# Attention tiles: the next queries turned before the third value product; and products of constants at the start

## The chip, the cores and the metric

The kernel runs on one core of a Trainium2 chip. Its engines run side by side and wait for each other by semaphores: TensorE (PE in the profile; PEld is its weight load), VectorE (DVE), ScalarE (ACT), GpSimd (POOL), and SyncE (SP), whose queue issues the DMAs. The metric is the device time of one execution in microseconds; three runs of the kernel before gave 1705.12, 1705.86 and 1711.52, median 1705.86.

## The reference

One step of a two-layer decoder on 2048 prompt tokens and 64 sample tokens (8 sequences of 8), width 1024, all in fp32:

```
# layer 0 (phase A, and the first half of phase B)
h = rms_norm(x, norm_a);  a, gl, z = split(h @ w_in_a, 3)
v = a * sigmoid(gl);      c = causal depthwise conv of v, 31 taps, + b_dw
x1 = x + (silu(layer_norm(c)) * silu(z)) @ w_out_a
# shared keys and values, queries, gate (the rest of phase B; the gate in phase C)
k, v = split(rms_norm(x1, norm_kv) @ w_kv);  k = rms_norm per head
q, z = split(rms_norm(x1, norm_b) @ w_in_b); q = rms_norm per head
# layer 1 (phase C), per block of 128 queries, over its own and the block before of keys
s = q k^T / 8 - slope * distance   (causal, window 128)
p = exp(s - m) / (sum + exp(sink - m));  o = p v
y = x1 + (o * silu(z)) @ w_out_b
```

There are 16 query heads on 4 key and value heads (groups of 4 query heads), head width 64.

## The kernel before

Each engine runs a program written out in order; what stands first in an engine's program and waits holds all behind it on that engine. Three phases follow each other: A (`phase_a`, to about 600 us) projects x for layer 0 and convolves; B (to about 1064 us, with a tail beside the first attention tile) norms, projects back, and makes keys, values and queries; C (`phase_c`) is the attention over 16 tiles of 128 queries (t = 0 to 15), and the sample tokens beside tiles 6 to 13.

**The start of phase A.** SyncE issues `load_x(0)`, the broadcast of the norm's gain, `load_x(1)`, unit 0 of the weights, `load_x(2)`, unit 1; then `load_x(3)`, which waits for the first x to be turned, eight small loads, and only then `load_unit(2)`. For each tile of x, ScalarE squares it (L514), GpSimd makes the root (L471, L473), VectorE scales it in place by root and gain (`scale_x`, L610), TensorE turns it in eight instructions (`turn_x`, L705), ScalarE copies the turned tile (`cut_hi`, L520) and VectorE the remainder (`cut_lo`, L616). The weights of a unit are cut by ScalarE (`split_hi`, L526) and VectorE (`split_lo`, L620). VectorE's program has `split_lo(2)` ahead of `scale_x(3)`. TensorE's first product group follows the first two turned tiles.

**A tile of phase C**, in the order of TensorE's program (`body`, L2387), where four groups of heads kv = 0 to 3 each have scores (`qk`, L2334), a turn of the exponentials P (`turn_p`, L2342) and a value product (`pv`): `pv` first turns two pieces of the gate (L2351), for which it waits for the group before to be multiplied out (`o_done`), then waits for P (`pt_ready`) and multiplies (L2357). Between these stand the gate's projection of this tile (`z`, L121 on `c_ht`) and the output projection of the tile before (`out`, L121 on `c_ot`). The tile ends: second half of `out`, `pv` of group 2 (the third value product), `turn_p` of group 3, the turn of the next tile's queries (`turn_q`, L2258), the turn of its keys (`turn_k`, L2264), `pv` of group 3 (the fourth). The next tile begins with `qk` of its group 0, which waits for queries and keys to be copied; in tiles 6 to 13 two turns of cached keys (L2294) stand before it.

What goes on beside that: after each value product ScalarE copies the turned gate (`copy_gate`, L1894), VectorE multiplies (`gated`, L2077), and only behind that in VectorE's program stands the copy of the next group's turned P (`parted`, L2054), for which `pv` waits. ScalarE copies the turned queries (`queries`, L1865) and keys (`keys`, L1871 and L1872; two copies where the next tile is even, one where it is odd).

**Tile 0** differs: it has no `out`; the gate of the sample tokens is projected there (`decode_z`, L130), and before `turn_q(1)` TensorE waits for VectorE to read its second half (`d_dve` at 3, VectorE L2089), since both use the same bank.

Of the kernel before, what the change touches and what calls it, by code (L numbers as in the profile page):

```python
# [14 lines left out]
P = 128  # L15
D = 1024
# [17 lines left out]
LN_EPS = 1e-5  # L34
# [234 lines left out]
def phase_a(nc, io, g, ctx):  # L269
# [5 lines left out]
    with ExitStack() as reused:  # L275
# [71 lines left out]
        def sync(sp, load_first, load_gate, load_second, load_x1, load_keys):  # L347
            def load_x(t):
                after(sp, xt_done, t - 2)
                n = rows_of(t)  # L350
                sp.dma_start(x[t % 3][0:n], io.x_sample if n == DEC else token_rows(io.x_prompt, t, n)).then_inc(x_in[t % 3], 16)
# [21 lines left out]
                sp.dma_start(g.vnew_d[b * P:(b + 1) * P, :], vbuf[:, b % 2, HIST + SEQ:HIST + TOK]).then_inc(vnew_out, 16)  # L373

            load_x(0)
            sp.dma_start(gain[:, :], io.norm_a.rearrange("(a d) -> a d", a=1).broadcast_to([P, D])).then_inc(gain_in, 16)
            load_x(1)
            load_unit(0)
            load_x(2)
            load_unit(1)  # L380
# [75 lines left out]
        def gpsimd(pool):  # L456
            pool.memset(g.half[:, :], -0.5).then_inc(ident_made, 1)
            pool.memset(g.rms_eps[:, :], RMS_EPS)
            pool.memset(g.share[:, :], 1.0 / D)
            pool.memset(g.ln_eps[:, :], LN_EPS).then_inc(ident_made, 1)  # L460
            pool.memset(g.ident[:, :], 0.0).then_inc(ident_made, 1)
            pool.wait_ge(ident_made, 3)
            pool.affine_select(out=g.ident[:, :], in_=g.ident[:, :], compare_op=ALU.not_equal, fill=1.0, base=0,
                               pattern=[[-1, P]], channel_multiplier=1).then_inc(ident_made, 1)
            pool.memset(vbuf[:, 0, 0:HIST], 0.0).then_inc(hist_zero, 1)

            def rms(t):
                n, q = rows_of(t), t % 2
                pool.wait_ge(ss_ready, t + 1)
                after(pool, xs_ready, t - 1)  # L470
                pool.tensor_tensor(ms[0:n, q:q + 1], ss[0:n, q:q + 1], g.rms_eps[0:n, 0:1], ALU.add).then_inc(ms_ready, 1)  # L471
                pool.wait_ge(ms_ready, t + 1)
                pool.tensor_tensor(rstd[0:n, q:q + 1], ms[0:n, q:q + 1], g.half[0:n, 0:1], ALU.pow).then_inc(rstd_ready, 1)  # L473

            def add_product(m):

                n, i = divmod(m, PTAPS - 1)
                i += 1
                _, t0, t1 = piece(n)
                out = csum[:, slot_of(n), 0:t1 - t0]  # L480
                pool.wait_ge(prod_ready, PTAPS * n + i + 1)
                if i == 1:
                    if n in (1, 2):
                        pool.wait_ge(hist_out, 16)
                    after(pool, c_out[slot_of(n)], 16 * (n // 3 + (n == pieces - 1)))
                    pool.tensor_tensor(out, prod[:, PTAPS * n % RING, 0:t1 - t0], prod[:, (PTAPS * n + 1) % RING, 0:t1 - t0], ALU.add).then_inc(prod_added, 1)  # L486
                    return
                pool.wait_ge(prod_added, m)
                pool.tensor_tensor(out, prod[:, (PTAPS * n + i) % RING, 0:t1 - t0], out, ALU.add).then_inc(prod_added, 1)  # L489

            for t in range(4):
                rms(t)
            added = 0
            for i in range(count):
                while added < plan.adds_by[i]:
                    add_product(added)
                    added += 1
                for t in range(2, ALL - 2):
                    if plan.cut_at[t] == i:
                        rms(t + 2)  # L500
                if i == plan.state_at + 3:
                    pool.wait_ge(st_t, 2)
                    pool.memset(vbuf[:, 1, 0:HIST], 0.0).then_inc(hist_zero, 1)
            while added < pieces * (PTAPS - 1):
                add_product(added)
                added += 1
# [192 lines left out]
        def tensor(pe, turn_first, turn_back):  # L699
            def turn_x(t):  # L700
                n = rows_of(t)
                pe.wait_ge(xs_ready, t + 1)
                after(pe, lo_ready, t - 1)
                for k in range(KT):
                    last = pe.transpose(ps_t[t % 2][:, k, 0:n], x[t % 3][0:n, k * P:(k + 1) * P], g.ident[0:n, 0:n])  # L705
                last.then_inc(xt_done, 1)

            def turn_state():
                n = DB * HIST // 2
                pe.wait_ge(st_in, 32)  # L710
                pe.wait_ge(lo_ready, ALL)
                for h in range(2):
                    for k in range(KT):
                        last = pe.transpose(ps_t[h][:, k, 0:n], x[h][0:n, k * P:(k + 1) * P], g.ident[0:n, 0:n])
                    last.then_inc(st_t, 1)

            def turn_v(b):
                pe.wait_ge(v_ready, NCH * (b + 1))
                pe.wait_ge(st_copied, 2)
                cols = slice(b * P, (b + 1) * P)  # L720
                pe.transpose(flat_t[1][0:HIST + DEC, cols], vbuf[:, b % 2, SEQ:HIST + TOK], g.ident[:, :]).then_inc(vt_done, 1)

            def project_group(i, between=None):
                u, c = groups[i]
                n = CHUNKS[c]
                if i >= 4:
                    done = {GATE: sig_ready, VALUE: v_ready, ZGATE: z_copied}[kind[i - 4]]
                    pe.wait_ge(done, nth[i - 4] + 1)
                pe.wait_ge(u_lo, u + 1)
                pe.wait_ge(lo_ready, CTILES[c + 1])  # L730
                out = bank[i % 4][:, 0:n]
                for k in range(KT):
                    if k == KT // 2 and between is not None:
                        pe.wait_ge(vo_ready, 1)
                        between()
                    if k == KT // 2:
                        for t in range(ALL):
                            if plan.turn_at[t] == 2 * i + 1:
                                turn_x(t)
                    for a, e in ((0, 0), (0, 1), (1, 0)):  # L740
                        last = pe.matmul(out, wring[:, u % 3, a, k], xt[c][:, e, k, 0:n], start=(k == 0 and a == 0 and e == 0),  # L741
                                         stop=(k == KT - 1 and a == 1))
                last.then_inc(grp, 1)

            pe.wait_ge(ident_made, 4)
            for i in range(count):
                if i == 3:
                    pe.wait_ge(raw_in, 16 * (2 + VECS + 2))
                    pe.transpose(bank[3][:, 0:P], raw[:, 0], g.ident[:, :])
                    pe.transpose(bank[3][:, P:TAPS * KT], raw[0:TAPS * KT - P, 1], g.ident[0:TAPS * KT - P, 0:TAPS * KT - P])  # L750
                    pe.transpose(bank[3][:, 256:256 + VECS * KT], raw[0:VECS * KT, 2], g.ident[0:VECS * KT, 0:VECS * KT]).then_inc(cols_t, 1)
                for t in range(ALL):
                    if plan.turn_at[t] == 2 * i:
                        turn_x(t)
                if i == 3:
                    pe.wait_ge(cols_ready, 2)
                if i == plan.state_at:
                    turn_state()
                for b in range(KT):
                    if plan.vt_at[b] == i:  # L760
                        turn_v(b)
                if i == last_z(0, 4):
                    turn_back()
                project_group(i, turn_first if i == out_at[2] else None)
# [841 lines left out]
def phase_c(nc, io, g, ctx, prev):  # L1606
# [245 lines left out]
    def scalar(act):  # L1852
# [51 lines left out]
        def decode_tanh(half):  # L1904
            part = zd[:, half * HALF:(half + 1) * HALF]
            act.wait_ge(d_pe, 3 + half)
            act.activation(part, z_at[half][DEC:P], ACT.Copy).then_inc(d_act, 1)
            act.wait_ge(d_dve, 1 + 2 * half)
            act.activation(low[0], part, ACT.Tanh, scale=0.5).then_inc(d_act, 1)
# [37 lines left out]
        def body(t, r):  # L1947
# [38 lines left out]
            exps(t * KVH + 3, 1)  # L1986
            if first:
                decode_tanh(1)
            copy_gate(t * KVH + 2, 2)
            if first:  # L1990
                split(6)
            if not last:
                queries(t + 1)
                keys(t + 1, 1 - r)
            if isinstance(t, int) and t == TILES - 2:
                decode_cut()
# [256 lines left out]
    def tensor(pe):  # L2253
# [133 lines left out]
        def body(t, r):  # L2387
# [42 lines left out]
                decode_z(1)  # L2430
            else:
                out(t - 1, 1, isinstance(t, int) and t == 1)
            pv(t, 2, r, loads)
            turn_p(t, 3, 1)
            if first:
                pe.wait_ge(d_dve, 3)
            if not last:
                turn_q(t + 1)
                if not first:
                    pe.wait_ge(res_done, t * 2)  # L2440
                turn_k(t + 1, 1 - r)
# [144 lines left out]
```

## Time and profile before

| | |
|---|---|
| median of three runs | 1705.86 us |
| the profiled execution, own time | 1704.73 us |
| its span, first to last instruction | 1702.9 us |
| TensorE busy (PE), weight load (PEld) | 97%, 79% |
| VectorE, ScalarE, GpSimd busy | 75%, 46%, 38% |
| mean granted clock of TensorE | 0.992 |

The busy shares are means over phases with different limits. The chain that ended last, followed back from the end, gives 60% to TensorE and 22% to GpSimd, whose share lies in phase A; in phase C it stays on TensorE nearly throughout. Two readings of the page need care: matmuls are pipelined, so a row's duration overlaps the next row's, and the step from start to start is what an instruction costs in a stream; and an fp32 product that isn't a turn shows as two TensorE instructions.

### The profile page before, as it was taken

The numbers are of one execution on the slowest core, as the hardware profiler recorded it, in microseconds if no ns is written. First come the engines' busy times: TensorE is split into PE (matmuls) and PEld (weight loads), VectorE is DVE, ScalarE is ACT, GpSimd is POOL, SyncE is SP. The second block draws the span as 40 slices with busy tenths as digits, with TensorE's granted clock in tenths as the row PEclk, the third lists the DMA queues.
The fourth block names the chain that finished last, engine by engine and source line by source line (L and its number), as shares of the span: only waits on it lengthen the run. The fifth ranks groups of instructions, "written<-read, shape, count | busy, mean of one in ns | idle before, by whom it ended". The sixth has DMA issues, their size and how long they took to land.

```text
span 1702.9 us, 26944 instructions
## 1 busy us (share of the span) xinstructions
PE 1644.7 (97%) x10267; PEld 1349.6 (79%) x10267; DVE 1272.8 (75%) x1944; ACT 778.9 (46%) x1625; POOL 648.8 (38%) x504
## 2 busy tenths in 40 slices
PE   7999999999999988999999999978999999999998
PEld 6899888888898876888888888756777777777776
DVE  6479889898888657889889433567777777777774
ACT  6655555565554545443343333454333443333431
POOL 2489999999985304445444332200000000000000
PEclk9999999999999999999999999989999999999999
DMA  7411111121120555444454342744222233322311
GB/s 218 129 58 43 50 48 55 48 69 44 62 89 28 181 195 201 139 158 156 156 149 156 119 155 80 234 146 129 97 97 72 85 106 115 103 102 91 104 62 44
DMA packets 153722, 186.06 MB, mean 109 GB/s; under 512 B 51028, under 2 KB 116668, under 8 KB 149450
## 3 DMA queue, kind: packets, MB, share of 16 engines
q1 hardware_dynamic: 149274, 172.54, 31.8%
q10 hardware_dynamic: 4320, 11.80, 1.8%
q8 instruction: 82, 1.34, 0.3%
q14 instruction: 46, 0.38, 0.1%
HBM read 116.41 MB, written 70.72 MB: 110 GB/s over the span
## 4 chain that ended last, share of the span: by engine, by line
PE 60%; POOL 22%; DVE 7%; ACT 3%; DMA 3%; issue 3%; SPq 1%; POOLq 0%; DVEq 0%; ACTq 0%
POOL a_csum L489 21%; PE c_acc L121 19%; PE b_pso L121 15%; PE b_psq L121 9%; PE c_pso L2357 4%; PE a_ps L741 3%; DVE a_pst L639 3%; PE c_pss L2334 2%; PE c_psp L2342 2%; POOL a_csum L486 1%; PE b_pst L1510 1%; PE a_pst L705 1%; PE c_pso L2351 1%; DVE w L109 1%; PE c_pst L2258 1%
## 5 line engine op out<-in xcount | busy, mean ns | idle before, releaser
L741 PE MATMUL a_ps<-a_xt,a_wring 128*128 128x512 f32 (+3 forms) x2880 | 557.7, 354 | 9.5 <-ACT a_zo L551 6.4
L741 PEld LDWEIGHTS a_ps<-a_xt,a_wring 128*128 128x128 f32 x2880 | 495.0, 189 | 65.8 <-ACT a_zo L551 8.0
L489 POOL TENSOR_TENSOR a_csum<-a_prod,a_csum 128x704 f32<-128x704 f32 (+1 forms) x231 | 405.3, 1754 | 43.1 <-ACT a_prod L538 9.9
L639 DVE SCALAR_TENSOR_TENSOR a_pst<-a_vbuf,taps,a_pst 128x704 f32<-128x704 f32 (+1 forms) x338 | 314.1, 929 | 10.4
L538 ACT ACTIVATE a_prod<-a_vbuf,taps 128x704 f32<-128x704 f32 (+1 forms) x252 | 214.7, 863 | 166.5 <-POOL a_csum L489 154.9
L121 PE MATMUL c_acc<-w,c_ht 128*128 128x512 f32 x768 | 184.8, 396 | 3.0 <-DVE c_sz L2019 2.3
L121 PE MATMUL b_pso<-w,b_yt 128*128 128x512 f32 x768 | 182.2, 393 | 0.7 <-DVE b_yt L1312 0.7
L121 PEld LDWEIGHTS c_acc<-w,c_ht 128*128 128x128 f32 x768 | 142.8, 189 | 39.2 <-issue 10.3
L121 PEld LDWEIGHTS b_pso<-w,b_yt 128*128 128x128 f32 x768 | 141.9, 188 | 29.5 <-DVE b_yt L1312 1.1
L1886 ACT ACTIVATE c_es<-c_es 128x4 f32<-128x4 f32 x64 | 13.1, 205 | 198.4 <-DVE c_es L2044 198.4
L121 PE MATMUL b_psq<-b_w,b_ht 128*128 128x512 f32 x384 | 94.9, 403 | 4.5 <-DVE b_w L109 4.5
L1888 ACT ACTIVATE c_s<-c_s,c_nm 128x128 f32<-128x128 f32 x256 | 98.8, 387 | 0.1
L121 PE MATMUL b_pso<-w,b_ht 128*128 128x512 f32 x384 | 91.4, 394 | 3.4 <-issue 3.4
L121 PE MATMUL b_psq<-w,b_ht 128*128 128x512 f32 x384 | 91.4, 393 | 0.0
L2031 DVE SCALAR_TENSOR_TENSOR c_s<-c_dist,c_pss 128x256 f32<-128x256 f32 (+1 forms) x256 | 88.1, 406 | 2.9 <-PE c_pss L2334 2.9
L121 PEld LDWEIGHTS b_psq<-b_w,b_ht 128*128 128x128 f32 x384 | 72.7, 193 | 21.2 <-DVE b_w L109 6.3
L121 PE MATMUL c_acc<-w,c_ot 128*128 128x512 f32 x360 | 85.9, 394 | 2.9 <-issue 2.9
L1400 DVE SCALAR_TENSOR_TENSOR b_conv<-b_three,taps,b_conv 128x704 f32<-128x704 f32 x90 | 87.1, 967 | 2.0
L121 PEld LDWEIGHTS b_pso<-w,b_ht 128*128 128x128 f32 x384 | 73.0, 191 | 19.0 <-issue 3.6
L121 PE MATMUL c_acc<-b_w,c_ot 128*128 128x512 f32 x360 | 86.0, 394 | 1.1 <-issue 1.1
L121 PEld LDWEIGHTS b_psq<-w,b_ht 128*128 128x128 f32 x384 | 71.0, 188 | 15.6
L121 PEld LDWEIGHTS c_acc<-b_w,c_ot 128*128 128x128 f32 x360 | 66.4, 188 | 17.9 <-issue 3.9
(247 smaller groups left out, 2242.3 us busy)
## 6 DMA issues: line engine op xcount, KB each, us to landing
ht_d<-b_ht SPq DMA_DIRECT2D x16, 1024.0 KB, 5.0
c_ht<-ht_d SPq DMA_DIRECT2D x16, 1024.0 KB, 5.0
a_stage<-in_w_in_a SPq DMA_DIRECT2D x24, 512.0 KB, 4.2
a_x<-in_x_prompt SPq DMA_DIRECT2D x16, 512.0 KB, 3.6
b_cz<-c_d SPq DMA_DIRECT2D x16, 512.0 KB, 5.6
b_cz<-z_d SPq DMA_DIRECT2D x16, 512.0 KB, 4.1
b_x<-in_x_prompt SPq DMA_DIRECT2D x16, 512.0 KB, 4.2
x_d<-b_x SPq DMA_DIRECT2D x16, 512.0 KB, 2.6
```

What stands on the lines that cost most here:

```text
L109: dve.scalar_tensor_tensor(g.wslot[m][:, 1, k], g.stage[:, piece % g.stages], gain_of(gain, k), f32(g.wslot[m][:, 0, k]), ALU.mult, ALU.su ...
L121: last = pe.matmul(out, xt[:, a, k, 0:n], w[:, b, k], start=(k == 0 and a == 0 and b == 0), stop=(k == KT - 1 and b == 1))
L489: pool.tensor_tensor(out, prod[:, (PTAPS * n + i) % RING, 0:t1 - t0], out, ALU.add).then_inc(prod_added, 1)
L538: act.activation(prod[:, m % RING, 0:t1 - t0], vbuf[:, b % 2, t0 + k:t1 + k], ACT.Identity, scale=wcol(k, b), bias=bcol(b) if i == 0 else ...
L639: dve.scalar_tensor_tensor(part if k == DTAPS - 1 and not last else here, vbuf[:, b % 2, t0 + k:t1 + k], wcol(k, b), part if k == 0 else h ...
L741: last = pe.matmul(out, wring[:, u % 3, a, k], xt[c][:, e, k, 0:n], start=(k == 0 and a == 0 and e == 0), stop=(k == KT - 1 and a == 1))
L1400: dve.scalar_tensor_tensor(cw, win, w, cw, ALU.mult, ALU.add).then_inc(old_step, 1)
L1888: ins = act.activation(s[:, b, j], s[:, b, j], ACT.Exp, bias=nm[:, b, j:j + 1], accum_out=den[:, b, j:j + 1])
L2031: ins = dve.scalar_tensor_tensor(to, far, -slope[kv * GROUP + j], given, ALU.mult, ALU.add)
L2334: ins = pe.matmul(to, qt[rows, h // 2, part * SUB:(part + 1) * SUB], keys[:, span_of(t, part)], start=True, stop=True)
L2342: ins = pe.transpose(ps_p[:, b, j], s[:, b, j], g.ident[:, :])
L2357: ins = pe.matmul(ps_o[e * HD:(e + 1) * HD, 0:2 * P], v[:, half, kv * HD:(kv + 1) * HD], pt[:, half, 2 * e:2 * e + 2], start=(half == 0), ...
```

## The change

Two parts. In phase C, TensorE turns the next tile's queries right after the second half of `out`, ahead of the third value product, and ScalarE copies them ahead of that product's gate copy; the turn of the keys stays where it was. In phase A, TensorE multiplies a constant column (`g.share`, spread to 128x128) 22 times before the first x is there, twice after the first turned tile and seven times before the first product group; GpSimd fills that column earlier by one place, and SyncE loads the second x ahead of the gain.

```diff
@@ sync
             load_x(0)
+            load_x(1)
             sp.dma_start(gain[:, :], io.norm_a...).then_inc(gain_in, 16)
-            load_x(1)
             load_unit(0)
@@ gpsimd
-            pool.memset(g.share[:, :], 1.0 / D)
-            pool.memset(g.ln_eps[:, :], LN_EPS).then_inc(ident_made, 1)
+            pool.memset(g.ln_eps[:, :], LN_EPS)
+            pool.memset(g.share[:, :], 1.0 / D).then_inc(ident_made, 1)
@@ tensor, phase A
+            def warm(n):
+                ones = g.share[:, :].broadcast_to([P, P])
+                for _ in range(n):
+                    pe.matmul(bank[3][:, 0:P], ones, ones, start=True, stop=True)
+            pe.wait_ge(ident_made, 2)
+            warm(22)
             pe.wait_ge(ident_made, 4)
...
                         turn_x(t)
+                        if t == 0:
+                            warm(2)
+                if i == 0:
+                    warm(7)
@@ scalar, phase C
             exps(t * KVH + 3, 1)
             if first:
                 decode_tanh(1)
+            if not last:
+                queries(t + 1)
             copy_gate(t * KVH + 2, 2)
             if first:
                 split(6)
             if not last:
-                queries(t + 1)
                 keys(t + 1, 1 - r)
@@ tensor, phase C
                 out(t - 1, 1, isinstance(t, int) and t == 1)
-            pv(t, 2, r, loads)
-            turn_p(t, 3, 1)
             if first:
                 pe.wait_ge(d_dve, 3)
             if not last:
                 turn_q(t + 1)
+            pv(t, 2, r, loads)
+            turn_p(t, 3, 1)
+            if not last:
                 if not first:
                     pe.wait_ge(res_done, t * 2)
                 turn_k(t + 1, 1 - r)
```

On TensorE, at the end of a tile of phase C (c_ot: attention output; c_sz: gate; c_pt, c_v: P and values; c_q, c_kd: next queries and keys), before:

```order
L121 MATMUL c_acc<-w,c_ot 128x512 x24
L2351 MATMUL c_pso<-ident,c_sz 128x128 x2
L2357 MATMUL c_pso<-c_pt,c_v 64x256 x4
L2342 MATMUL c_psp<-ident,c_s 128x128 x4
L2258 MATMUL c_pst<-ident,c_q 128x128 x8
L2264 MATMUL c_acc<-ident,c_kd 128x128 x4
L2351 MATMUL c_pso<-ident,c_sz 128x128 x2
L2357 MATMUL c_pso<-c_pt,c_v 64x256 x4
L2334 MATMUL c_pss<-c_kt,c_qt 32x160 x16
```

Now, at the same place (the line numbers are those of the changed kernel: L2364 and L2370 are `pv`, L2355 `turn_p`, L2271 `turn_q`, L2277 `turn_k`, L2347 `qk`):

```order
L121 MATMUL c_acc<-w,c_ot 128x512 x24
L2271 MATMUL c_pst<-ident,c_q 128x128 x8
L2364 MATMUL c_pso<-ident,c_sz 128x128 x2
L2370 MATMUL c_pso<-c_pt,c_v 64x256 x4
L2355 MATMUL c_psp<-ident,c_s 128x128 x4
L2277 MATMUL c_acc<-ident,c_kd 128x128 x4
L2364 MATMUL c_pso<-ident,c_sz 128x128 x2
L2370 MATMUL c_pso<-c_pt,c_v 64x256 x4
L2347 MATMUL c_pss<-c_kt,c_qt 32x160 x16
```

The eight turns of the queries moved from between the third and the fourth value product to ahead of the third; nothing else changed place.

On TensorE at the start of the program (a_x: tiles of x; a_xt, a_wring: turned x and weights), before:

```order
L705 MATMUL a_pst<-ident,a_x_59 128x128 x8
L705 MATMUL a_pst<-ident,a_x_60 128x128 x8
L741 MATMUL a_ps<-a_xt_49,a_wring 128x256 x12
L705 MATMUL a_pst<-ident,a_x_63 128x128 x8
L741 MATMUL a_ps<-a_xt_49,a_wring 128x256 x12
L705 MATMUL a_pst<-ident,a_x_59 128x128 x8
```

Now, with the products of the constant column (share):

```order
L749 MATMUL a_ps<-share 128x128 x22
L705 MATMUL a_pst<-ident,a_x_59 128x128 x8
L749 MATMUL a_ps<-share 128x128 x2
L705 MATMUL a_pst<-ident,a_x_60 128x128 x8
L749 MATMUL a_ps<-share 128x128 x7
L741 MATMUL a_ps<-a_xt_49,a_wring 128x256 x12
L705 MATMUL a_pst<-ident,a_x_63 128x128 x8
```

The three L749 rows are new; the others stand in the order of before.

## Rows read from the trace of the kernel before

**Rows 1.** Waits of TensorE, 1175 to 1703 us: who, whom, us, times, longest
```profile
PE c_pss L2334 <- issue: 1.4, 3, 0.5
```

**Rows 2.** Timeline of TensorE at the end of tile 3: start, us, engine, line, times
```profile
1253.80 1.08 PE L2357 MATMUL c_pso<-c_pt,c_v 128*64 128x256 f32 x8
...
1255.31 1.04 PE L2258 MATMUL c_pst<-ident,c_q 128*128 128x128 f32 x8
1256.18 0.60 PE L2264 MATMUL c_acc<-ident,c_kd 128*128 128x128 f32 x4
...
1257.02 1.08 PE L2357 MATMUL c_pso<-c_pt,c_v 128*64 128x256 f32 x8
1258.57 0.78 PE L2334 MATMUL c_pss<-c_kt,c_qt 64*32 64x160 f32 x32 [0.46 <-issue]
```

**Rows 3.** Timeline of VectorE at the same place; in brackets idle time, its releaser
```profile
1255.35 0.42 DVE L2077 TENSOR_TENSOR c_sz<-c_pso,c_sz 128x256 f32<-128x256 f32 x1 [0.97 <-ACT c_sz L1894]
1255.69 1.28 DVE L2054 TENSOR_TENSOR c_pt<-c_psp,c_causal 128x512 f32<-128x512 f32 x2
```

**Rows 4.** Timeline of ScalarE at the same place
```profile
1256.38 1.11 ACT L1865 ACTIVATE c_qt<-c_pst,b_qscale 128x1024 f32<-128x1024 f32 x1 [1.06 <-PE c_pst L2258]
...
1257.87 0.60 ACT L1872 ACTIVATE c_kt<-c_acc 128x512 f32<-128x512 f32 x1
```

**Rows 5.** Timeline of TensorE at the end of tile 15, which turns no queries
```profile
1677.01 1.08 PE L2357 MATMUL c_pso<-c_pt,c_v 128*64 128x256 f32 x8
...
1679.13 0.41 PE L2351 MATMUL c_pso<-ident,c_sz 128*128 128x128 f32 x2 [0.45 <-DVE c_sz L2077]
1680.24 1.08 PE L2357 MATMUL c_pso<-c_pt,c_v 128*64 128x256 f32 x8 [0.69 <-DVE c_pt L2054]
```

**Rows 6.** Timeline of TensorE from tile 7 to 8, and from 8 to 9
```profile
1398.28 0.44 PE L2294 MATMUL c_pst<-ident,c_stg 128*128 128x128 f32 x2
1398.81 0.78 PE L2334 MATMUL c_pss<-c_kt,c_qt 64*32 64x160 f32 x32
...
1433.99 0.44 PE L2294 MATMUL c_pst<-ident,c_stg 128*128 128x128 f32 x2
1434.36 0.77 PE L2334 MATMUL c_pss<-c_kt,c_qt 64*32 64x160 f32 x32
```

**Rows 7.** Timeline of TensorE in tile 0
```profile
1141.93 0.66 PE L2342 MATMUL c_psp<-ident,c_s 128*128 128x128 f32 x4 [0.59 <-ACT c_s L1888]
1144.60 1.09 PE L2258 MATMUL c_pst<-ident,c_q 128*128 128x128 f32 x8 [2.01 <-DVE c_early L2089]
```

**Rows 8.** Windows: stretch, length, busy us (instructions) by engine, PEclk, DMA share, GB/s
```profile
8.00:15.60 7.60, 3.90 (x16) 3.12 (x16) 4.78 (x4) 5.39 (x8) 0.95 (x3) 1.00 0.92 283
15.60:20.10 4.50, 4.42 (x21) 4.46 (x22) 3.86 (x4) 2.70 (x4) 2.17 (x3) 1.00 0.53 179
...
1116.00:1126.00 10.00, 6.67 (x65) 4.36 (x63) 8.38 (x21) 3.69 (x13) 2.33 (x1) 1.00 0.39 107
1126.00:1133.00 7.00, 4.49 (x21) 3.37 (x18) 2.50 (x9) 3.02 (x13) 0.00 (x0) 0.51 1.07 304
```

**Rows 9.** Timeline of all engines, 17 to 22 us
```profile
17.23 1.07 ACT L526 ACTIVATE a_wring<-a_stage 128x1024 fp32r<-128x1024 f32 x1
...
18.38 1.89 PE L705 MATMUL a_pst<-ident,a_x 128*128 128x128 f32 x8
19.71 1.28 DVE L610 SCALAR_TENSOR_TENSOR a_x<-a_x,a_rstd,a_gain 128x1024 f32<-128x1024 f32 x1
...
21.54 1.04 PE L705 MATMUL a_pst<-ident,a_x 128*128 128x128 f32 x8
```

**Rows 10.** The load of weight unit 2 by itself: duration ns, start us, and landing
```profile
L357 SPq DMA_DIRECT2D a_stage<-in_w_in_a x1: 401/401/401, 13.4 to 13.4; - x1
...
DMA to landing us min/median/max: 3.8/3.8/3.8
```

**Rows 11.** A product with the constant column in phase B, all of the program
```profile
L1499 PE MATMUL b_psc<-share,b_cz x28: 270/273/323, 670.3 to 1039.1; 128*128 128x128 f32 x26, 128*64 128x128 f32 x2
```

## The prediction

> **What bounds the kernel now.** I read four views, in this order: the waits of TensorE in phase C, the timelines of three engines at the end of one tile, the same place in the last tile, and then the start and tile 0 by timeline and windows. From tile 1 on phase C is a stream of TensorE: of waits for the next tile's first scores the trace lists three, 1.4 us together [rows 1], and there is no slack in which a later wait could be lost. A microsecond that TensorE waits at a tile's end is therefore a microsecond of the kernel. What matters is who is late there.
>
> At the end of tile 3 the third value product starts at 1253.80 and the fourth at 1257.02, 3.22 us later [rows 2]. Between them TensorE turns P of group 3, the queries (1255.31 to 1256.18, so 0.87 us by starts) and the keys. The fourth product needs its P copied by VectorE. That copy starts at 1255.69, straight behind the multiplication of group 2 at 1255.35, which had stood idle 0.97 us for ScalarE's copy after the third product; it takes 1.28 us and ends at 1256.97 [rows 3]. TensorE starts 0.05 us after that, having found work up to the last tenth. So two paths of equal length run from the third to the fourth product: TensorE's own work, and third product, ScalarE copy, VectorE multiply, VectorE copy. Tile 15 shows the second path bare. There no queries or keys are turned, TensorE waits 0.45 us and then 0.69 us for VectorE, and the fourth product starts at 1680.24, 3.23 us after the third at 1677.01 [rows 5]. The path of 3.23 us has nothing to do with how much TensorE does meanwhile.
>
> **Phase C, tiles 1 to 14.** The change takes the 0.87 us of query turns out of the stretch between the two products and puts them ahead of the third. The third starts 0.87 us later, the bare path of 3.22 us follows it as before, and the fourth starts 0.87 us later, with TensorE idle for about that long. The cover was the point of the old place. ScalarE does not lengthen the path: its query copy takes 1.11 us from 0.03 us after the turns [rows 4], and the third product with its two gate turns runs longer than that, so `copy_gate` finds ScalarE free. Fourteen tiles have the change: 14 x 0.87 = 12.2 us lost.
>
> What it gives back is the wait for the keys. In tile 3 the last key copy ends at 1257.87 + 0.60 = 1258.47 and the scores start at 1258.57 after 0.46 us idle [rows 2, 4]. With the queries copied early the keys are done before the fourth product is, and that wait goes; what is late next is the copy of P above. The listed waits of this kind are worth 1.4 us [rows 1]. In the even tiles with cached keys ahead of the scores a shorter one shows: 0.53 us from start to start into tile 8 against 0.37 us into tile 9 [rows 6], 0.16 us in four tiles, 0.6 us. Together 2.0 us gained, and the net of the steady tiles is 12.2 - 2.0 = +10.2 us. Bounds: +8 us if each tile hides 0.15 us of the new wait somewhere, +12.2 us if nothing of the old one comes back.
>
> **Phase C, tile 0.** Here TensorE waits 2.01 us for VectorE before it turns the queries, and the third value product and the turn of P at 1141.93 are done by then [rows 7]. Now both stand behind that wait. At full clock they add at most their own length, 0.65 us for the turn of P and about as much for the product (half of a full tile's 1.08 us, since one block of keys, not two, with its gate turns): 1.3 us, of which ScalarE's copies after it may hide some; I take 0.9 us. The product ended at 1141.93 - 0.59 = 1141.34; with it and the turn moved away TensorE has nothing from before 1140.7 to 1144.6, about 4 us. The clock gate speaks here: after a stretch with 6.67 us busy in 10 the granted clock was 0.51 in the next 7 us, which is the lower level of 1.2 GHz for nearly all of them [rows 8]. Falling again at 1144 would double the 3.1 us that TensorE needs to the next scores (about the 3.2 us of rows 2). Bounds for tile 0: 0 and 1.3 + 3.1 = 4.4 us; I take +1.9 us, nearer the low end, because the lower level need not cover all of those 3.1 us.
>
> The Trainium skill, "TensorE: Matmul & The Clock Gate", section "HAM oscillation — how this bites in real kernels", says that TensorE's clock is dropped again when a burst of products ends in a wait that is long enough. The trace agrees in rows 8; by that rule alone tile 0 costs the upper half of my bounds, without it 0.9 us.
>
> **The start.** The column of PEclk shows 1.00 from the first us, but durations show otherwise: eight turns took 1.89 us at 18.38 and 1.04 us at 21.54 [rows 9], so TensorE ran at 1.2 GHz until about 20 and at 2.4 GHz after. The 22 products are fp32; the constant product of phase B shows 28 instructions for 14 products [rows 11], so 22 are 44 instructions, at most 44 x 1.89/8 = 10.4 us at the low level, about 8 if the clock rises on the way. They start near 1 us on an engine that waits for the first x, so they end between 8 and 11.4 us. The first x is turned about 9, if anything later than before, since its scaling needs the gain, which now lands in the second x's place: in the upper half of that stretch the products would hold it up by up to 2 us, which the bound of +1.5 below nearly takes in.
>
> What the start can give back is limited by a load. VectorE scales x tile 3 at 19.71, right behind the split of weight unit 2, whose ScalarE half starts at 17.23 [rows 9], and that unit was issued at 13.37 and landed 3.8 us later, at 17.2 [rows 10]. Its issue hangs on the first turned x and eight small loads behind it, so it comes no earlier. Tile 3 is turned at 21.54, only 0.55 us after its scaling ended at 20.99 [rows 9]. So a faster TensorE gains 0.4 us there, and up to 1 us a little later, then sits on the same load. Against it, of the 4.2 us by which TensorE's busy time shrinks (rival 1) what isn't gained is idle time, some 3 us of it ahead of tile 3, and the clock may fall there once; at half speed for 3 us that is up to +1.5 us. Value -0.5 us, bounds -4.2 (below) and +1.5. After that phase A runs as before, earlier or later by that amount: the order of every engine is unchanged, and GpSimd's long chain starts from TensorE's first groups. The moved fill of GpSimd costs nothing: two fills of one column each change places.
>
> **The sum.** 1704.73 us of the profiled execution (span 1702.9 and 1.8 around it), +10.2 +1.9 -0.5 = 1716.3 us. The median of the runs stands 1.1 us above that execution, so I predict 1717 us, 0.65% slower.
>
> **Rivals.**
> 1. The warm start is worth what it looks like. From 8.0 to 20.1 us TensorE was busy 3.90 + 4.42 = 8.3 us at the low level [rows 8]; at the high one it needs half, 4.2 us less, and if nothing but TensorE were on the path the whole program would start 4.2 us sooner. With 10.2 and 0.9 us in phase C: 1705.9 + 6.9 = 1713. For it: no TensorE instruction waits between 15.6 and 20.1. Against it: rows 9 and 10. The same page's section "What's actually happening" says that the low clock is the default and activity lifts it, which is what this part of the change relies on; rows 9 bear it out, and by it alone the start would be this rival's.
> 2. The new wait is only half as long: the copy of P slips ahead, say 0.4 us a tile. Then 14 x 0.4 - 2.0 + 1.9 - 0.5 = +5, 1711 us. Against it: VectorE's order puts the copy behind the multiplication, and tile 15 shows the path whole.
> 3. Not slower: the fourth product does not wait for P at all and the change does what it says, early queries and no wait for keys. Then only -2.0 us and the start's -0.5 to -4.2 count: 1705.9 - 2.5 = 1703 us, at best 1700. It decides where the copy of P is ready 3.1 us or less after a third product that has less work behind it. For it: 0.05 us is a small margin to read a cause from. Against it: 0.69 us of waiting on just that copy in tile 15 [rows 5].
> 4. Worse: the clock also falls in tiles of the steady part or at the start twice: +15 us or more, 1721.
>
> **Chances.** Forecast 0.68, rival 1 0.12, rival 2 0.08, rival 3 0.07, rival 4 0.05. What can be told from no change is 0.5%, 8.5 us. Slower by more: most of the forecast (0.55 of 0.68, since its low end at +8 lies within), rival 4 and a little of rival 1, 0.61. Within: 0.34. Faster: the best of rival 3 with luck, 0.05. The range leaves out rival 3 and the far end of rival 4: 1707 to 1722; the forecast's own is 1712 to 1721.
>
> **What would show it.** In the changed profile, at the end of tiles 1 to 14, TensorE's value product must show idle time of some 0.7 to 0.9 us released by VectorE's copy of P, the distance of third to fourth product must still be 3.2 us, and the idle time before the next scores must be gone. Tile 0 should show about 4 us of idle TensorE and a granted clock under 1 soon after. The first x should be turned in about 1 us, not twice that, tile 3 should be turned near 21 us, and `split_hi` of unit 2 should still start near 17. The prediction is wrong if the distance of the two products shrinks to 2.4 us, or if tile 3 of x is turned before 19 us.

## The result, and the profile after

The changed kernel took 1716.95 us (median of 9 runs, 1714.06 to 1720.5) against 1703.55 us (median of 9, 1700.54 to 1711.52) for the kernel before on the same chip: ratio 1.0072, 95% interval 1.006 to 1.0084, so 10.2 to 14.3 us slower. The profiled execution took 1716.68 us, its span is 1714.9 us, 12.0 more than that of before. I split this difference at four marks of the two timelines.

| stretch (mark: instruction in the trace) | before | after | difference | forecast |
|---|---|---|---|---|
| start, to GpSimd's first sum | 64.89 | 65.30 | +0.4 | -0.5 |
| from there to the first scores of phase C | 1038.10 | 1036.54 | -1.6 | 0 |
| first scores to the end of tile 1's output product | 81.68 | 84.93 | +3.25 | +1.9 |
| end of that product in tile 1 to its end in tile 15 | 492.19 | 502.01 | +9.8 | +10.2 |

The four add to +11.9. The second row has no edit in it. TensorE's clock fell at other places there (586.7, 631.1, 648.2 and 1088.5 us before; 646.8 alone after), and I put the difference down to that. In the third row the profile of before has a fall at 1112.4 us, ahead of the end of tile 0's decode product (`decode_z`), that the other lacks; from that end on the row costs 4.0 us and not 3.25.

**The steady tiles.** The first view is the timeline of TensorE at the end of tile 3 in the changed kernel (start, us, engine, line, tiles; in brackets the idle time before and what ended it), the counterpart of [rows 2]:

```profile
1256.82 1.03 PE L2271 MATMUL c_pst<-ident,c_q 128*128 128x128 f32 x8
1257.69 0.38 PE L2364 MATMUL c_pso<-ident,c_sz 128*128 128x128 f32 x2
1258.00 1.08 PE L2370 MATMUL c_pso<-c_pt,c_v 128*64 128x256 f32 x8
1259.02 0.66 PE L2355 MATMUL c_psp<-ident,c_s 128*128 128x128 f32 x4
1259.51 0.60 PE L2277 MATMUL c_acc<-ident,c_kd 128*128 128x128 f32 x4
1260.12 0.41 PE L2364 MATMUL c_pso<-ident,c_sz 128*128 128x128 f32 x2
1261.22 1.08 PE L2370 MATMUL c_pso<-c_pt,c_v 128*64 128x256 f32 x8 [0.70 <-DVE c_pt L2067]
1262.24 0.77 PE L2347 MATMUL c_pss<-c_kt,c_qt 64*32 64x160 f32 x32
```

The two value products are 3.22 us apart, as before. In place of the query turns (0.87 us by starts, from 1256.82 to 1257.69) stands idle time: 0.70 us that VectorE's copy of P ends, and some 0.17 us ahead of the gate turns at 1260.12. The next scores start 1.02 us after the fourth product, not 1.55. VectorE at the same place, to compare with [rows 3]:

```profile
1259.55 0.42 DVE L2090 TENSOR_TENSOR c_sz<-c_pso,c_sz 128x256 f32<-128x256 f32 x1 [1.84 <-ACT c_sz L1906]
1259.89 1.28 DVE L2067 TENSOR_TENSOR c_pt<-c_psp,c_causal 128x512 f32<-128x512 f32 x2
```

It works on the same chain behind ScalarE's gate copy and only waits longer for it, 1.84 us where it was 0.97. The multiplication starts 1.55 us after the third product in both kernels. The view that groups TensorE's waits from 1175 us on (who, whom: us, times, longest) shows it for all tiles (14, and tile 15, which had this wait before); the row of [rows 1] is gone from the list:

```profile
PE c_pso L2370 <- DVE c_pt L2067: 10.4, 15, 0.7
PE c_acc L121 <- issue: 2.4, 1, 2.4
```

**Tile 0.** TensorE's timeline, to compare with [rows 7]:

```profile
1142.68 1.97 PE L2271 MATMUL c_pst<-ident,c_q 128*128 128x128 f32 x8 [4.34 <-DVE c_early L2102]
1144.44 0.64 PE L2364 MATMUL c_pso<-ident,c_sz 128*128 128x128 f32 x2
1145.01 1.12 PE L2370 MATMUL c_pso<-c_pt,c_v 128*64 128x256 f32 x4
...
1149.68 1.09 PE L2347 MATMUL c_pss<-c_kt,c_qt 64*32 64x256 f32 x32
```

The idle time is 4.34 us, and the eight turns behind it take 1.97 us, nearly twice the 1.09 of before. The windows (length, busy us by engine, then the granted clock of TensorE, the DMA share and GB/s) show why:

```profile
1138.30:1141.70 3.40, 0.04 (x1) 0.00 (x0) 2.05 (x6) 2.15 (x10) 0.00 (x0) 1.00 0.00 0
...
1141.70:1148.50 6.80, 5.82 (x26) 4.41 (x28) 2.73 (x5) 3.60 (x6) 0.00 (x0) 0.50 0.24 80
```

After 3.4 us with 0.04 us of work the granted clock is 0.50, the level of 1.2 GHz.

**The start.** TensorE's timeline, to compare with [rows 9]:

```profile
1.01 7.12 PE L749 MATMUL a_ps<-share 128*128 128x128 f32 x44 [1.01 <-POOL share L460]
8.96 1.06 PE L705 MATMUL a_pst<-ident,a_x 128*128 128x128 f32 x8 [0.83 <-DVE a_x L610]
...
15.77 1.09 PE L705 MATMUL a_pst<-ident,a_x 128*128 128x128 f32 x8
16.62 1.67 PE L741 MATMUL a_ps<-a_xt,a_wring 128*128 128x256 f32 x12
20.84 1.09 PE L705 MATMUL a_pst<-ident,a_x 128*128 128x128 f32 x8 [2.55 <-DVE a_x L610]
```

The 44 instructions are done at 8.13 us and the clock is up: eight turns take 1.06 us at 8.96. That is 0.9 us later than before (8.02), and it is not the products that hold them up but VectorE's scaling, which now waits for the gain (it started at 6.59 before):

```profile
7.52 2.48 DVE L610 SCALAR_TENSOR_TENSOR a_x<-a_x,a_rstd,a_gain 128x1024 f32<-128x1024 f32 x2 [7.52 <-DMA a_gain<-in_norm_a]
```

By the third tile this is made up: the turns that stood at 18.38 stand at 15.77, 2.6 us earlier. Tile 3 of x is turned only 0.7 us earlier, after 2.55 us of idle time. Its cause is ScalarE's wait for the load of unit 2, where `split_hi` starts at 17.27 against 17.23:

```profile
17.27 1.06 ACT L526 ACTIVATE a_wring<-a_stage 128x1024 fp32r<-128x1024 f32 x1 [1.79 <-DMA a_stage<-in_w_in_a]
```

And behind that idle time the granted clock falls, so that the rest is given back (tile 5 of x is turned at 28.43, before at 28.29):

```profile
20.10:28.30 8.20, 7.46 (x51) 7.46 (x52) 5.80 (x7) 4.99 (x9) 1.77 (x4) 0.79 0.18 67
```

### The profile page after: what moved, and what is told of

It is laid out like the page before. It is cut to its first block, busy times and chain, and to the rows that moved or that the text cites. A ratio compares the mean times of both kernels' runs of the same rounds, so it can differ in the third digit from the quotient of the medians.

```text
span 1714.9 us, 27068 instructions
## 1 busy us (share of the span) xinstructions
PE 1651.9 (96%) x10329; PEld 1354.4 (79%) x10329; DVE 1273.8 (74%) x1944; ACT 781.9 (46%) x1625; POOL 646.9 (38%) x504
## 4 chain that ended last, share of the span: by engine, by line
PE 59%; POOL 24%; DVE 7%; DMA 3%; issue 3%; ACT 3%; SPq 1%; POOLq 0%; DVEq 0%; ACTq 0%
POOL a_csum L489 22%; PE c_acc L121 19%; PE b_pso L121 14%; PE b_psq L121 9%; PE c_pso L2370 4%; PE a_ps L741 3%; PE c_pss L2347 2%; DVE a_pst L639 2%; POOL a_csum L486 2%; PE c_psp L2355 1%; DVE c_pt L2067 1%; DVE w L109 1%; PE b_pst L1522 1%; PE c_pst L2271 1%; PE a_pst L705 1%
```

## The experiments

"The way through tile 0" below is the time from the end of tile 0's decode product (`decode_z`) to the end of tile 1's output product; it is 44.43 us before and 48.43 us after. "The steady sum" is the last row of the table.

### 1. Phase C's part alone

The two phase C hunks of the diff, nothing of the start.

> Phase C's part of the change alone, the start of before. Theory (the turns of the queries were the cover of VectorE's path to the fourth value product): all of the loss is here: 14 tiles x 0.87 us less 2.3 us of key waits = +9.8 us, and some 3 us in tile 0, where TensorE stands idle and its clock falls: +13 us over before, about as slow as the changed kernel. Third to fourth product 3.22 us, 0.69 us idle before the fourth. Rival (the products of constants at the start cost the time, by the clock or by the later first tile): within 2 us of before.

Measured: 1717.84 us, ratio to before 1.0081 (1.0066 to 1.0096). Steady sum 502.07 us. The list of waits has the row of the changed kernel again:

```profile
PE c_pso L2358 <- DVE c_pt L2055: 10.4, 15, 0.7
```

This part alone loses as much as the whole change, as far as the intervals tell.

### 2. Phase A's part alone

The other three hunks.

> Phase A's part alone, the order of phase C as before. Theory (the start sits on the load of weight unit 2, whatever TensorE's clock is): 0 to +1 us against before; x tile 3 turned near 20.8 us, the first add of GpSimd's chain within 0.5 us of before's 64.9. Rival (the faster first turns reach the end): 3 to 4 us faster than before, GpSimd's first add near 61.

Measured: 1706.47 us, ratio 1.0009 (0.9996 to 1.0023). Tile 3 of x is turned at 20.92 us after 2.68 us of idle time, tile 5 at 28.57, GpSimd's first sum starts at 65.20 (64.89 before), and the clock falls between 21.4 and 24.8 us. A gain of 3 to 4 us is excluded. On the other side 1.5 us of loss, with an interval from -0.7 to +3.9, can't be told from none. The products and the two exchanged loads were not run apart.

### 3. The whole change, but tile 0 in the old order

```diff
-            if first:
-                pe.wait_ge(d_dve, 3)
-            if not last:
+            if not last and not first:
                 turn_q(t + 1)
             pv(t, 2, r, loads)
             turn_p(t, 3, 1)
+            if first:
+                pe.wait_ge(d_dve, 3)
+                turn_q(t + 1)
```

and the same on ScalarE.

> The whole change, but tile 0 of phase C in the old order on TensorE and ScalarE. Theory (tile 0 loses by TensorE's 4 us of idling and the fallen clock after it): 2 to 4 us faster than the changed kernel, +9 to +10 us over before; no granted clock under 1 right after tile 0's wait, the 14 tiles unchanged. Rival (tile 0 is hidden by VectorE's and ScalarE's splits beside it): the same time as the changed kernel.

Measured: 1718.48 us (4 runs), ratio 1.0082 (1.0065 to 1.0099). The gain was not there. Tile 0 had its old order and the old wait of 2.01 us, but in this execution the clock fell at 1144.3 us all the same, and the way through tile 0 was 48.13 us. An interval of 2.9 us either way cannot show an effect of 2 us; experiments 9 to 11 take the question up.

### 4. ScalarE's order alone undone

```diff
-            if not last:
-                queries(t + 1)
             copy_gate(t * KVH + 2, 2)
             if first:
                 split(6)
             if not last:
+                queries(t + 1)
                 keys(t + 1, 1 - r)
```

> The whole change on TensorE, but ScalarE copies the queries behind the gate copy of group 2, as before. Theory (the path third product, gate copy, multiplication, copy of P is bare because TensorE's turns no longer lie on it; ScalarE's order does not matter): time of the changed kernel within 1 us in the tiles, third to fourth product 3.22 us, 0.69 us idle. Rival (the early query copy on ScalarE holds up the gate copy): third to fourth product falls below 3.2 us and the kernel is back within 3 us of before.

Measured: 1719.22 us, ratio 1.0091 (1.0076 to 1.0106); steady sum 502.00, distance of the products 3.22 us, idle time 0.69 us:

```profile
1260.22 1.08 PE L2369 MATMUL c_pso<-c_pt,c_v 128*64 128x256 f32 x8
...
1263.44 1.08 PE L2369 MATMUL c_pso<-c_pt,c_v 128*64 128x256 f32 x8 [0.69 <-DVE c_pt L2066]
```

Where ScalarE copies the queries makes no difference: the cost is TensorE's order.

### 5. Phase A's part, and unit 2 issued ahead of the eight small loads

```diff
+            load_unit(2)
+            load_x(4)
...
-            load_unit(2)
-            load_x(4)
```

> Phase A part alone (constants multiplied at the start, second x ahead of the gain), and with it weight unit 2 and the fifth x are issued ahead of the eight small loads instead of behind them; phase C as before. Theory (the start sits on the load of unit 2, so a faster TensorE alone gains nothing): the unit is issued at about 11.8 us instead of 13.4, lands near 15.5, VectorE scales x tile 3 near 18 and TensorE turns it near 19.3 instead of 20.9; x tile 5 and GpSimd's first sum come some 1.5 to 2.5 us earlier than before (28.3 and 64.9), TensorE's clock stays up because its idle time ahead of tile 3 shrinks from 2.55 to about 1.1 us, and the kernel is 1.5 to 3 us faster than before (1700.6 to 1702 against a before of 1703.5). Rival (the load isn't what holds; the small loads moved back hold as much, or phase B absorbs it): tile 3 at 20.9 or the sum at 65, and the time as with the phase A part alone, within 0.1% of before.

Measured: 1706.01 us against 1706.46 in this batch, ratio of the runs 0.9992 (0.9981 to 1.0002). The profile shows the theory's chain. The load is issued at 11.8 us, ScalarE splits it 0.8 us earlier, TensorE turns tile 3 at 20.04 after a shorter wait, the clock stays up, and tile 5 stands at 26.13 us, 2.2 us earlier than before:

```profile
20.04 1.09 PE L705 MATMUL a_pst<-ident,a_x 128*128 128x128 f32 x8 [1.72 <-DVE a_x L610]
20.89 3.11 PE L741 MATMUL a_ps<-a_xt,a_wring 128*128 128x256 f32 x24
...
26.13 1.04 PE L705 MATMUL a_pst<-ident,a_x 128*128 128x128 f32 x8
```

GpSimd's first sum starts at 63.01 (-1.9 us). The load now takes 4.6 us to land, not 3.8, which is why tile 3 missed the 19.3 us expected. So in this execution the load was what held the start; experiment 8 has the same start in another. In the time 1.4 us less is the middle of an interval that just reaches no change.

### 6. The keys turned ahead of the queries

The kernel before, but in tiles 1 to 14 `turn_k` and `keys` stand ahead of `turn_q` and `queries`, all of them still between the third and the fourth value product.

```diff
             if first:
                 pe.wait_ge(d_dve, 3)
-            if not last:
                 turn_q(t + 1)
+            if not last:
                 if not first:
                     pe.wait_ge(res_done, t * 2)
                 turn_k(t + 1, 1 - r)
+            if not last and not first:
+                turn_q(t + 1)
```

> The kernel before with one exchange in tiles 1 to 14: the next tile's keys are turned and copied ahead of the next tile's queries, both still between the third and the fourth value product; tile 0 and the start as before. Theory (what the old place loses is only the wait for the keys, and the queries' turns are the cover of the path through P): distance of third and fourth product stays 3.22 us with no wait ahead of the fourth, the waits of 0.46, 0.15 and 0.05 us before the next scores go, these start 1.0 us (no decode) or 1.38 us (decode) after the fourth product in all tiles, the 14 steady tiles take 490 instead of 492.2 us, and the time is 2 us (0.12%) less than before. Rival (the queries, now last, take the place of the keys as what is late): the wait before the scores stays at 0.2 us or more and the time is the same.

Measured: ratio 0.9987 (0.9978 to 0.9995), 0.9 to 3.8 us less than before. Steady sum 490.59. At the end of tile 3:

```profile
1253.52 1.08 PE L2359 MATMUL c_pso<-c_pt,c_v 128*64 128x256 f32 x8
...
1256.74 1.08 PE L2359 MATMUL c_pso<-c_pt,c_v 128*64 128x256 f32 x8
1257.80 0.78 PE L2336 MATMUL c_pss<-c_kt,c_qt 64*32 64x160 f32 x32
```

3.22 us between the products without a wait, and the scores 1.06 us behind. The wait for keys was worth having; it did not need the cover to be given away. A part of the rival holds: in four tiles (5, 7, 9, 11) the scores start 1.49 us after the product, not 1.38, so 0.1 us of a wait, now for the queries, is left there.

### 7. Half of the query turns moved

```diff
+            if not last and not first:
+                turn_q(t + 1, 0, 4)
             pv(t, 2, r, loads)
...
-                turn_q(t + 1)
+                turn_q(t + 1, 0 if first else 4, KT)
```

> The kernel before with four of the next tile's eight query turns moved ahead of the third value product in tiles 1 to 14, the other four where all eight were; ScalarE's copies in their old order. Theory (a path of 3.22 us through ScalarE and VectorE, which the turns between the products cover up to the last tenth): half of the turns uncover half of it; TensorE waits 0.35 to 0.43 us for the copy of P ahead of the fourth product, whose distance from the third stays 3.22; every tile that does not get the key wait back loses 0.43 us, the 14 tiles 3 to 5 us in all, and the time is 0.2 to 0.3% more than before. Rival (it is the early place of the whole block that costs, not the cover): no wait or the whole 0.7 us.

Measured: ratio 1.0026 (1.0013 to 1.0038), steady sum 496.23, 4.0 us more than before. The end of tile 3:

```profile
1255.38 1.08 PE L2358 MATMUL c_pso<-c_pt,c_v 128*64 128x256 f32 x8
...
1258.60 1.08 PE L2358 MATMUL c_pso<-c_pt,c_v 128*64 128x256 f32 x8 [0.46 <-DVE c_pt L2054]
```

The distance is still 3.22 us. Half of the turns leave 0.46 us of wait and cost 4.0 us in all; the whole block leaves 0.70 and costs 9.8. The cost goes with the work taken from between the products.

### 8. Experiments 5 and 6 together

> Both counter-versions together: constants multiplied at the start with weight unit 2 and the fifth x issued ahead of the eight small loads, and in tiles 1 to 14 the keys ahead of the queries, both between the third and fourth value product. Theory: the two gains add, 3.5 to 5 us less than before (about 1699 against 1703.5), faster than both kernels. Rival (one of the two gives nothing): 2 us or less. Tile 0 is in the old order here, as in the two runs with one part each, so its granted clock shows besides whether falls there come and go without any edit of that tile.

Measured: 1701.97 us, ratio 0.9974 (0.9961 to 0.9988), 2.0 to 6.7 us less than before and so faster than both kernels. Steady sum 490.57. Its profiled execution was the slowest of its 12 runs (1709.35 us), with clock falls at the start (20.8 us) and in tiles 0 and 1; tile 0 has no edit here. Its start is that of experiment 5, and in this execution it gained nothing. Unit 2 was issued at 12.3 us and took 4.9 us to land, so ScalarE splits it no earlier than before and TensorE turns tile 3 at half the clock:

```profile
17.25 1.06 ACT L526 ACTIVATE a_wring<-a_stage 128x1024 fp32r<-128x1024 f32 x1 [1.26 <-DMA a_stage<-in_w_in_a]
20.82 1.97 PE L705 MATMUL a_pst<-ident,a_x 128*128 128x128 f32 x8 [2.02 <-DVE a_x L610]
```

Tile 5 is turned at 28.50 and GpSimd's first sum starts at 65.50 us, 0.6 later than before. So one of the two profiles with the early load gained 1.9 us by that mark and the other none.

### 9 to 11. Tile 0 by itself, and both kernels profiled again

The first is the kernel before with tile 0 alone in the new order, the other two are unedited.

```diff
+            if first:
+                pe.wait_ge(d_dve, 3)
+                turn_q(t + 1)
             pv(t, 2, r, loads)
             turn_p(t, 3, 1)
-            if first:
-                pe.wait_ge(d_dve, 3)
-            if not last:
+            if not last and not first:
                 turn_q(t + 1)
```

> The kernel before with tile 0 alone in the new order (queries of tile 1 turned ahead of its third value product and copied ahead of the gate); tiles 1 to 15 and the start as before. Theory of the prediction (the order of tile 0 puts product and turn behind VectorE's wait and lets the clock fall): TensorE idle 4.3 us ahead of the turns, the way from the end of tile 0's decode product to the end of tile 1's output product 46.5 to 48.5 us instead of 44.4, and the kernel 2 to 4 us (0.1 to 0.2%) slower than before. Theory formed since (the falls in tiles 0 and 1 come with either order, and between executions that fall, new and old order differ by 0.2 us): where the clock falls in the profile, the way is 48 us as with the old order, where it doesn't, under 45; the time is within 0.1% of before.

> A second profile of the kernel before, nothing edited. If the clock's falls in tiles 0 and 1 belong to the execution and not to an order, they may show here too (a fall between 1140 and 1150 us or between 1175 and 1185, and 46.5 to 48 us from the decode product's end to the end of tile 1's output product); if they belong to the change, the way is 44.4 us as in the first profile. The sum of tiles 2 to 15 is 492.2 us in either case.

> A second profile of the changed kernel, nothing edited. The sum of tiles 2 to 15 is 502.0 us again. If the falls in tiles 0 and 1 belong to the new order, the way from the decode product's end to the end of tile 1's output product is 48.4 us again with the clock at half speed from about 1141; if they belong to the execution, one or both may be missing and the way 44.5 to 46.5 us.

Measured: tile 0 alone gave 1708.56 us (12 runs, 1706.39 to 1711.28) against 1706.0 (17 runs, 1700.91 to 1709.94), ratio 1.0017 (1.0006 to 1.0028), so 1.0 to 4.8 us slower. Its way through tile 0 is 50.14 us, behind the same idle time as in the changed kernel:

```profile
1143.24 1.97 PE L2261 MATMUL c_pst<-ident,c_q 128*128 128x128 f32 x8 [4.35 <-DVE c_early L2092]
```

The second profile of the kernel before has the way at 48.54 us, where the first has 44.43. The instruction is that of [rows 7], with the same wait, at half the clock:

```profile
1144.17 1.97 PE L2258 MATMUL c_pst<-ident,c_q 128*128 128x128 f32 x8 [2.02 <-DVE c_early L2089]
```

Two stretches of that profile, on both sides of the fall:

```profile
1139.80:1143.30 3.50, 1.53 (x11) 0.62 (x8) 2.15 (x6) 2.13 (x10) 0.00 (x0) 1.00 0.00 0
1143.30:1150.10 6.80, 5.93 (x42) 4.51 (x50) 3.60 (x8) 4.54 (x9) 0.00 (x0) 0.50 0.24 77
```

The second profile of the changed kernel has 48.32 us, the idle time of 4.35 us, and the fall from 1144.8 us. Its steady sum is 502.13, that of the second profile of before 492.24.

All 13 profiles, by the order of tile 0:

| order of tile 0 | profiles | clock falls before the next scores | end of `decode_z` to the next scores, us | way through tile 0, us |
|---|---|---|---|---|
| old | before, 2, 6 | 0 of 3 | 8.00 to 8.01 | 44.43, 44.31, 46.50 |
| old | before again, 3, 5, 7, 8 | 5 of 5 | 8.80 to 9.63 | 47.80 to 48.54 |
| new | after, after again, 1, 4, 9 | 5 of 5 | 11.18 to 11.34 | 47.97 to 50.14 |

The mean of the way is 47.0 us in the eight profiles with the old order and 48.6 in the five with the new one. The way takes in a second place: all ten profiles with the fall in tile 0 have another in tile 1 (from 1175.9 to 1182.4 us), and so has experiment 6, whose way of 46.50 us shows what that one alone costs, some 2 us. Among the profiles that fall in tile 0 the orders are close: 48.1 us in the mean of the five old ones, 48.6 in that of the five new.

Both theories were half right. The time of tile 0 alone, 2.6 us more by the medians, is what the prediction's theory gave (2 to 4); the 0.1% of the other lies low in the interval. That the falls come with either order is what the other gave. With the old order the fall comes in some executions and not in others, which is why experiment 3 showed no gain in its one profile. With the new order it came in every profile, and no run of the 12 with tile 0 alone was as short as the quickest 11 of the 17 of before beside them. Five profiles are few; that the longer idle time makes the fall certain is the reading that fits, not one that was shown by itself.

## Why the prediction was right

The forecast of 1717 us (1716.3 + 1.1 = 1717.4, rounded) met the median of 1716.95, by the mechanism that it named. Term by term:

**Tiles 1 to 14, +10.2: measured +9.8.** The third product starts 1.02 us after the end of `out`, before it was 0.15, so 0.87 later as forecast, and the path of 3.22 us behind it did not shorten (experiments 1, 4, 7). The new wait was forecast as "about that long"; it is 0.87 us in two pieces, 0.70 for P and 0.17 for the gate multiplied out. The gain against it was a little larger than my 2.0 us: by the starts of the scores after the fourth product, 3 tiles gain 0.54, 4 tiles 0.17, and 3 tiles 0.05 us (1.06 to 1.01, which I did not count), together 2.4 us. 12.2 - 2.4 = 9.8. Reading tile 15 as the bare path was what decided: it gave the distance and the wait of 0.69 us that then stood in fourteen other tiles. Rivals 2 and 3 fall with this. Experiment 7 excludes another reading, that the early place costs as a whole.

**Tile 0, +1.9: measured +2.9 (1.0 to 4.8) by itself.** The idle time of 4.3 us and the clock below 1 behind it came as forecast. To the next scores the cost is 3.3 us, in the upper part of my bounds of 0 to 4.4. The step that failed is that I set this against one profile in which the clock happened not to fall. I held the fall for something that the change would add, while with the old order it was there in five of eight profiles. The prediction also took [rows 8] as a case of a long enough wait that drops the clock, and they aren't one. In the 10 us before that fall no wait is longer than 1.97 us (the row below, kernel before), and in the second profile of before the clock fell at 1143.3 us, little more than 1 us into the wait of 2.02:

```profile
1125.16 0.41 PE L2351 MATMUL c_pso<-ident,c_sz 128*128 128x128 f32 x2 [1.97 <-DVE c_sz L2077]
```

So the clock also falls here without the wait of 4 us to which the prediction tied it, and the change's average cost is less than the pair of traces shows (1.6 us by the means of the table, 4.0 by that pair).

**The start, -0.5: measured +1.5 (-0.7 to +3.9) by itself, +0.4 in the profile.** The chain was right: products done in about 8 us, the first x turned in about 1 us, tile 3 near 21 us, `split_hi` near 17. The loss was inside the bound, and its term was named: idle time ahead of tile 3, and the clock falls there once. I valued it as the less likely case, and that is the step that failed. All five profiles with the changed start have this fall (21.1 to 22.2 us; the two of the changed kernel, experiments 2 to 4), none of the six with the old start has it, and GpSimd's first sum starts at 65.44 us in the mean of the five, 65.05 in that of the six. Rival 1, 4.2 us of gain, is refuted by experiment 2, and experiment 5 shows what the faster start needs, a load that lands earlier. Experiment 8 shows that issuing it earlier does not always bring that.

**What the sum left out.** The pair of profiles has -1.6 us in a stretch that no edit touches, which I put down to clock falls there. It made up for what tile 0 and the start cost beyond their terms; the three parts measured by themselves add to 9.8 + 2.9 + 1.5 = 14.2 us, above the 12.3 measured for the whole (0.72% of 1703.55) but inside the intervals. The forecast also started too high: its three runs of before have their median at 1705.86 us, the nine at 1703.55, 2.3 us less, while the sum of 11.6 us was 1.8 short of the 13.4 between the two medians. The two errors cancel, so that the median fell within half a microsecond of the forecast is luck; the 10 us of the steady tiles aren't.

## What to carry to other kernels

Here work that an engine did between two steps of a chain through other engines, as long as that work, cost nothing there and its full 0.87 us ahead of the chain. So before moving such work, measure the bare chain: a tile at the edge of the loop that lacks this work shows it. If something else in that gap is late, exchange it with its neighbours inside the gap (keys ahead of queries, experiment 6) rather than moving the cover out. And the faster engine at the start gained nothing while the load that the next step waits for landed at its old time: look at that load first, and at when it lands, not only at when it is issued.

## What the runs showed of the hardware that was not expected

The same program, with the same instructions and waits, has TensorE's clock fall in tile 0 in one execution and not in another: 48.54 and 44.43 us for the same stretch, with the fall in tile 1 that comes with it, in two profiles of the kernel before. The spread of its nine runs is 1700.5 to 1711.5 us, and the granted clock goes with the time: of the 17 runs beside experiment 9 the quickest (1700.91 us) has a mean granted clock of 0.996, the slowest (1709.94) 0.989. TensorE's work ahead of it is the same: 1.53 of 3.50 us busy from 1139.80 in the one with the fall, and in the other, from 1140.23, the same eleven instructions:

```profile
1140.23:1143.73 3.50, 1.54 (x11) 0.62 (x8) 2.15 (x6) 2.13 (x10) 0.00 (x0) 1.00 0.00 0
```

What decides between them is open. The Trainium skill, "TensorE: Matmul & The Clock Gate", section "What's actually happening", says that the stretches in which the chip judges TensorE's activity run free of the program, so that the same kernel meets its clock changes at different places from run to run. The outcome here agrees with that; no run here shows that it is the cause. For a change of 2 us in such a kernel one pair of profiles shows the path, not the price; the price takes a dozen runs of each.
